# Stored expert weights of the first layer: one transfer for two value steps, and five row slots instead of six

## The chip, the cores and the metric

The kernel runs on one core of one Trainium2 chip. The metric is device time in microseconds, the median of the runs. A profiled execution is a run of its own, with its own time.

## What is computed

A first block of two layers and a second block follow each other; the change lies in the first block's retrieval of single-neuron experts. With `n` tokens of width 1024, 8 heads, 16 choices each and 16384 experts:

```python
q = (hb @ w_q).reshape(n, PEER_HEADS, 2, PEER_DK_HALF)
s = jnp.einsum('nhpk,pek->nhpe', q, keys)
v_top, i_top = lax.top_k(s, PEER_TOPK)
...
e = i1 * N_KEYS + i2
g = jax.nn.softmax(sc.astype(jnp.float32), axis=-1).astype(hb.dtype)
a = jax.nn.gelu(jnp.einsum('nhkd,nd->nhk', u_tab[e], hb)) * g
return jnp.einsum('nhk,nhkd->nd', a, v_tab[e])
```

In the first layer this is done for 512 tokens (256 of the input, 256 of the context), in the second for the 256 of the input.

## The kernel before, in words

The kernel doesn't gather experts token by token. `peer` (L1694) computes the scores of all 16384 experts for all tokens, multiplies them with a dense matrix that holds the softmax weight where an expert was chosen and zero elsewhere, and multiplies the result with all of `peer_v`. Everything is float32, split into a high and a low half, so each product is three matmuls.

Its loops, each over tiles of 256 experts (`U` = 64 of them), with one block of instructions per engine, written out in order:

- Score steps: PE multiplies a tile of `peer_u` with the tokens, ACT applies the gelu, SP stores the scores in DRAM (`K.scores`). Beside that, DVE picks the best 16 and builds the dense weights, which go to DRAM in blocks of tokens (`K.dense`).
- Value steps, `m` = 0 to 63. SP fetches a tile of `peer_v` (1 MB, `fetch`, L1838), the scores of the step (`pr_gs`, L1863) and the dense weights of the step (`pr_g`, L1864). DVE multiplies scores and weights (`multiply`: L2303 twice to add two halves, L2305), ACT rounds the product to its high half (`split_a`, L2131) and the value tile to its high half (`split_hi`, L2061), DVE makes the low halves (`split_v`, L2314, and L2344), and PE accumulates (`combine`): in the first layer 36 matmuls of 512 columns.

In the first layer (`parts` is true) the value steps treat 384 of the 512 tokens. The first 128 are done by gathering: POOL gathers their 128 chosen scores (`gather_score`, L1919) and then the 128 chosen rows of `peer_v` for each token, one row per token and gather, 512 KB at a time (`gather_value`, L1925), and DVE adds them up with their weights (`sum_value`, L2331), 128 sums spread over steps 8 to 63, two or three per step.

The dense weights of the first layer lie in 12 blocks of 32 tokens. For each block `b` and each of the 128 partitions `j`, `K.dense[b, j, :]` is a row of 8192 numbers, and the 128 numbers of a step are 512 B of it.

What sets the order: each engine runs its own list. SP's list in the value steps is, for each `m`, first the scores and weights of step `m + 2` (`fetch_weighted`), then the value tile of step `m + ring`. In the first layer `ring` is 3, and its wait (`used`) is for the end of `combine(m)`. So after the end of `combine(m)` the value tile, the scores and the weights of step `m + 3` are issued together. `fetch_weighted` waits until the step three before has been multiplied (`mulled`), since there are three slots of scores and three of weights. DVE's list per step: multiply, split the value tile, the sums, the low half of the product; DVE counts both transfers of a slot on one semaphore (`sg_in`). POOL's list alternates a value gather and a score gather; a value gather into a slot that was used before waits for the sum that read it (`v_summed`), with six slots.

Of the kernel before, what the change touches and what calls it, by code (L numbers as in the profile page):

```python
# [9 lines left out]
ALU = mybir.AluOpType  # L10
# [4 lines left out]
P = 128  # L15
# [19 lines left out]
PH, TOPK, NKEYS = 8, 16, 128  # L35
# [16 lines left out]
@contextmanager  # L52
def stage(K, *names):


    nc = K.nc
    turn = K.stages % 2
    K.stages += 1
    sems = K.sems[turn][0:len(names)]
    retired = K.sems[1 - turn]  # L60
    with nc.Block(no_gpsimd_drain=True) as block:  # L61
        @block.gpsimd
        def _(pool):
            pool.sem_clear(range(retired[0].num, retired[-1].num + 1))
        yield (block, *sems)
# [1628 lines left out]
def peer(K, l, hT, x, t0, held):  # L1694
# [14 lines left out]
    parts = pairs == 2  # L1709
# [19 lines left out]
    nb = dw // stored  # L1729
# [9 lines left out]
    def ada_after(m):  # L1739
        return m - ada_from if ada_from <= m < ada_from + n_ada else None  # L1740
# [4 lines left out]
    with ExitStack() as mem:  # L1745
        def sb(name, shape, dt=F32, scope=mem):
            return scope.enter_context(nc.sbuf_tensor(f"pr_{name}{l}", shape, dt))
        act_s = sb("s", [P, 3, 2, tw])
        n_sel, v_slots, first_sum = PH * TOPK, 6, 8
        if parts:  # L1750
            sel_w = sb("sel_w", [P, n_sel])
            sel_row, sel_score = sb("sel_row", [P, n_sel], U32), sb("sel_score", [P, n_sel], U32)
# [38 lines left out]

        aslots = 2
        gs = sb("gs", [P, 3, 2, dw])
        gw = sb("g", [P, 3, nb, 2 * 64])
        a = sb("a", [P, aslots, 2, dw])
        a2 = sb("ahi", [P, aslots, 2, dw], F32R), sb("alo", [P, aslots, 2, dw], F32R)
        tail = ExitStack()
# [6 lines left out]
        if parts:  # L1804
# [4 lines left out]
                 "step", "shifted", "exped", "picked", "turned", "chosen", "hots_made", "hots_hi", "hots_lo", "paired", "copied",  # L1809
                 "g_stored0", "g_stored1", "s_stored0", "s_stored1", "s_stored2", "ada_in0", "ada_in1", "row_ready", "row_copied",  # L1810
                 "row_stored0", "row_stored1", "mod_in", "sg_in0", "sg_in1", "sg_in2", "v_lo", "mulled", "a_hi", "a_lo", "used", "outed", "scaled", "rows_in",
                 "selected", "sel_in0", "sel_in1", "sel_in2", "sel_in3", "v_in0", "v_in1", "v_in2", "v_in3", "v_in4", "v_in5", "v_summed"]
        with stage(K, *names) as \
                (block, w_in0, w_in1, w_in2, w_in3, keys_in, hi_ready, lo_ready, lo_later, scored, freed, key_scored, sc_copied, topped,
                 step, shifted, exped, picked, turned, chosen, hots_made, hots_hi, hots_lo, paired, copied,
                 g_stored0, g_stored1, s_stored0, s_stored1, s_stored2, ada_in0, ada_in1, row_ready, row_copied,
                 row_stored0, row_stored1, mod_in, sg_in0, sg_in1, sg_in2, v_lo, mulled, a_hi, a_lo, used, outed, scaled, rows_in,
                 selected, sel_in0, sel_in1, sel_in2, sel_in3, v_in0, v_in1, v_in2, v_in3, v_in4, v_in5, v_summed):
            w_in, g_stored, s_stored = (w_in0, w_in1, w_in2, w_in3), (g_stored0, g_stored1), (s_stored0, s_stored1, s_stored2)
            ada_in, row_stored, sg_in = (ada_in0, ada_in1), (row_stored0, row_stored1), (sg_in0, sg_in1, sg_in2)  # L1820
            sel_in, v_in = (sel_in0, sel_in1, sel_in2, sel_in3), (v_in0, v_in1, v_in2, v_in3, v_in4, v_in5)
            chunk = n_sel // len(sel_in)

            @block.sync
            def _(sp):
# [33 lines left out]
                def fetch_weighted(m):  # L1859
                    sp.wait_ge(s_stored[m % 3], 16 * (m // 3 + 1))  # L1860
                    if m >= 3:
                        sp.wait_ge(mulled, m - 2)
                    sp.dma_start(gs[:, m % 3, :, :], K.scores[m, :, 0:2 * tw].rearrange("p (e t) -> p e t", e=2)[:, :, off:tw]).then_inc(sg_in[m % 3], 16)  # L1863
                    sp.dma_start(gw[:, m % 3, :, :], K.dense[0:nb, :, m * 128:(m + 1) * 128].rearrange("b j n -> j b n")).then_inc(sg_in[m % 3], 16)  # L1864

                sp.dma_start(keys[:, :, :], K.dram["peer_keys"][l]).then_inc(keys_in, 16)
                lag = PH + 1 + ring
                for n in range(ring, first_v + lag - PH):
                    if n < first_v + ring:
                        fetch(n)  # L1870
                    m = n - lag
# [11 lines left out]
                    c = ada_after(m + lead)  # L1883
                    if c is not None:
                        fetch_ada(c)
                    c = ada_after(m)
# [6 lines left out]
                for m in range(U):  # L1893
                    if m + 2 < U:
                        fetch_weighted(m + 2)
                    if first_v + m + ring < first_v + U:
                        fetch(first_v + m + ring)
                    if m == U - 8 and not nxt:
                        sp.dma_start(x[:, 0:2, :], K.dram["mem"].rearrange("(t p) d -> p t d", p=P)).then_inc(rows_in, 16)
                    if m == 4:  # L1900
                        for s in range(2):
                            sp.dma_start(mod5[:, s, :], K.ada[l, s:s + 1, 5 * D:6 * D].broadcast_to([P, D])).then_inc(mod_in, 16)
# [4 lines left out]
            @block.gpsimd  # L1907
            def _(pool):
                def split_lo(n):
                    s = n % slots  # L1910
                    pool.wait_ge(hi_ready, n)
                    pool.tensor_tensor(w_lo[:, n % ring, :, :], wt[:, n % ring, :, :], w_hi[:, s, :, :].bitcast(F32),  # L1912
                                       ALU.subtract).then_inc(lo_ready, 1)

                for n in range(1, on_pool):
                    split_lo(n)

                def gather_score(j):
                    pool.indirect_dma_start(sel_s[:, j:j + 1], None, K.scores.rearrange("m p (n o) -> (m p n) o", o=1),  # L1919
                                            bass.IndirectOffsetOnAxis(ap=sel_score[:, j:j + 1], axis=0)).then_inc(sel_in[j // chunk], 16)  # L1920

                def gather_value(j):
                    if j >= v_slots:
                        pool.wait_ge(v_summed, j - v_slots + 1)
                    pool.indirect_dma_start(v_rows[:, j % v_slots, :], None, K.dram["peer_v"][l],  # L1925
                                            bass.IndirectOffsetOnAxis(ap=sel_row[:, j:j + 1], axis=0)).then_inc(v_in[j % v_slots], 16)

                if parts:
                    pool.wait_ge(selected, 1)
                    pool.wait_ge(row_copied, n_ada)  # L1930
                    for s in range(2):
                        pool.wait_ge(g_stored[s], 16 * (nb // 2))
                    for s in range(3):
                        pool.wait_ge(s_stored[s], 16 * ((U + 2 - s) // 3))
                    for j in range(chunk):
                        gather_score(j)
                    for j in range(n_sel):
                        gather_value(j)
                        if j + chunk < n_sel:
                            gather_score(j + chunk)  # L1940
# [227 lines left out]
            def _(dve):  # L2168
# [123 lines left out]
                            make_hots(g)  # L2292

                def multiply(m):
                    dve.wait_ge(sg_in[m % 3], 32 * (m // 3 + 1))
                    if m >= aslots:
                        dve.wait_ge(a_hi, m - aslots + 1)
                        dve.wait_ge(a_lo, m - aslots + 1)
                    if parts:
                        sums = a[:, m % aslots, :, :].rearrange("p e (b t) -> p b e t", t=stored)  # L2300
                        both_halves = gw[:, m % 3, :, :].rearrange("p b (e h t) -> p b e h t", e=2, h=2)
                        for e in range(2):
                            last = dve.tensor_tensor(sums[:, :, e, :], both_halves[:, :, e, 0, :], both_halves[:, :, e, 1, :], ALU.add)  # L2303
                        chain(last)
                        dve.tensor_tensor(a[:, m % aslots, :, :], a[:, m % aslots, :, :], gs[:, m % 3, :, :], ALU.mult).then_inc(mulled, 1)  # L2305
                        return
                    dve.tensor_tensor(a[:, m % aslots, :, :].rearrange("p e (b t) -> p e b t", t=64),
                                      gs[:, m % 3, :, :].rearrange("p e (b t) -> p e b t", t=64),
                                      gw[:, m % 3, :, :].rearrange("p b (e t) -> p e b t", t=64), ALU.mult).then_inc(mulled, 1)

                def split_v(m):
                    n = first_v + m
# [3 lines left out]

                def weigh(c):
                    cols = slice(c * chunk, (c + 1) * chunk)
                    dve.wait_ge(sel_in[c], 16 * chunk)
                    chain(dve.tensor_tensor(sel_a[:, cols], sel_w[:, cols], sel_s[:, cols], ALU.mult))  # L2320

                def sum_value(j):
# [28 lines left out]
                for o in range(outs):  # L2351
                    t, c = divmod(o, 2)
# [99 lines left out]
def first_layer(K, l, x, s_cols, cmp_bias):  # L2452
# [6 lines left out]
    with ExitStack() as mem:  # L2459
# [16 lines left out]
        with ExitStack() as rows:  # L2476
# [14 lines left out]
            with ExitStack() as over:  # L2491
# [3 lines left out]
        merge_out(K, l, x, (yT, y_lo), room, gm[:, :, :].rearrange("p (s a) c -> p s (a c)", s=2), ft[:, :, :].rearrange("p t c -> p (t c)"), hT, tiles, streams,  # L2495
                  held.ahead(K.dram["peer_w_q"][l]))
        peer(K, l, hT, x, t0, held)


# [1351 lines left out]
```

## Time and profile before

| | |
|---|---|
| time, median of 3 runs | 4358.7 us (4357.69 to 4365.27) |
| profiled execution, its own time | 4376.78 us |
| its span | 4375.0 us |
| PE busy | 3984.4 us (91%) |
| DVE busy | 2747.7 us (63%) |
| ACT busy | 1756.1 us (40%) |
| POOL busy | 786.5 us (18%) |
| DMA, whole span | 858.34 MB in 520773 packets, mean 196 GB/s |

Busy time is that of an engine's own instructions; issuing a DMA isn't counted as busy. An engine's idle time carries the name of what ended it. The granted clock of TensorE is 1.00 at 2.4 GHz and 0.50 at 1.2 GHz. The DMA share is the time that packets took on the 16 DMA engines together; it can be a little over 1 in a short stretch.

### The profile page before, as it was taken

Reading aid. Unit: us, or ns where it says so; the run is one execution under the profiler, and the core shown is the slowest. Engines: PE = TensorE matmul, PEld = TensorE weight load, DVE = VectorE, ACT = ScalarE, POOL = GpSimd, SP = SyncE. Lnnn points to the kernel's source line nnn. Section 1 sums busy time; section 2 is a strip of 40 time slices with the busy share of each in tenths; the row PEclk is TensorE's granted clock in tenths of the full one; section 3 lists DMA queues with packets and bytes.
Section 4 is the critical chain, followed back from the end, with each engine's and each line's share of the span. In section 5 each row is a group of like instructions: output and inputs, shape, how many; then the busy total and the mean of one; then the engine's idle time right before and its main releaser. Section 6 shows DMA issues by size and latency. Waiting matters only on the chain. (4 is left out here: it accounts for less than half of the span.)

```text
span 4375.0 us, 61084 instructions
## 1 busy us (share of the span) xinstructions
PE 3984.4 (91%) x24438; PEld 3468.0 (79%) x24438; DVE 2747.7 (63%) x5244; ACT 1756.1 (40%) x2260; POOL 786.5 (18%) x386
## 2 busy tenths in 40 slices
PE   7999899999999888878889899999997988888798
PEld 5876788788878767666778899997887977878697
DVE  5725668899412577777765688745665745643664
ACT  3433233477433222222255444544444523543453
POOL 2222034200000655542243320000000030000000
PEclk9999999999999989988899999999998979998999
DMA  6421224377884999999444366778885401645264
GB/s 244 141 94 60 93 87 136 125 287 298 315 286 157 295 304 329 339 323 300 135 135 140 139 202 218 250 281 279 288 290 172 154 1 58 190 144 162 71 188 138
DMA packets 520773, 858.34 MB, mean 196 GB/s; under 512 B 26661, under 2 KB 388325, under 8 KB 499721
## 3 DMA queue, kind: packets, MB, share of 16 engines
q1 hardware_dynamic: 497962, 787.25, 53.7%
q0 software_dynamic: 22528, 67.19, 4.3%
q8 instruction: 194, 3.18, 0.3%
q14 instruction: 89, 0.73, 0.1%
HBM read 734.21 MB, written 120.14 MB: 195 GB/s over the span
## 5 line engine op out<-in xcount | busy, mean ns | idle before, releaser
L113 PE MATMUL bank<-hThi_l,pr_whi 128*128 128x512 f32 (+1 forms) x2304 | 785.5, 341 | 17.1 <-DVE pr_wlo L2179 6.9
L113 PE MATMUL bank<-hTlo_l,pr_whi 128*128 128x512 f32 (+1 forms) x2304 | 777.7, 338 | 0.0
L113 PE MATMUL bank<-hThi_l,pr_wlo 128*128 128x512 f32 (+1 forms) x2304 | 777.2, 337 | 0.0
L113 PE MATMUL bank<-pr_whi,pr_ahi 128*128 128x512 f32 x1280 | 518.8, 405 | 116.9 <-DVE pr_alo L2344 113.6
L2061 ACT ACTIVATE pr_whi<-pr_w 128x2048 fp32r<-128x2048 f32 x270 | 516.3, 1912 | 133.3 <-DMA pr_w<-peer_v_in 130.6
L113 PE MATMUL bank<-pr_wlo,pr_ahi 128*128 128x512 f32 x1280 | 513.9, 401 | 0.0
L113 PE MATMUL bank<-pr_whi,pr_alo 128*128 128x512 f32 x1280 | 513.0, 401 | 0.0
L113 PEld LDWEIGHTS bank<-hThi_l,pr_whi 128*128 128x128 f32 x2304 | 440.3, 191 | 67.0 <-POOL pr_wlo L1912 8.3
L113 PEld LDWEIGHTS bank<-hThi_l,pr_wlo 128*128 128x128 f32 x2304 | 439.6, 191 | 45.9
L113 PEld LDWEIGHTS bank<-hTlo_l,pr_whi 128*128 128x128 f32 x2304 | 440.4, 191 | 42.7
L2179 DVE TENSOR_TENSOR pr_wlo<-pr_w,pr_whi 128x2048 fp32r<-128x2048 f32 x102 | 233.5, 2290 | 339.6 <-ACT pr_whi L2061 339.4
L113 PEld LDWEIGHTS bank<-pr_whi,pr_ahi 128*128 128x128 f32 x1280 | 250.4, 196 | 182.9 <-issue 115.9
L2075 ACT ACTIVATE pr_s<-bank 128x512 f32<-128x512 f32 (+1 forms) x256 | 125.2, 491 | 522.9 <-PE bank L113 505.6
L2131 ACT ACTIVATE pr_ahi<-pr_a 128x768 fp32r<-128x768 f32 (+1 forms) x128 | 94.7, 740 | 554.8 <-DVE pr_a L2305 250.4
L2314 DVE TENSOR_TENSOR pr_wlo<-pr_w,pr_whi 128x2048 fp32r<-128x2048 f32 x128 | 292.4, 2284 | 17.6 <-ACT pr_whi L2061 17.6
L113 PEld LDWEIGHTS bank<-pr_whi,pr_alo 128*128 128x128 f32 x1280 | 249.7, 195 | 54.3
L113 PEld LDWEIGHTS bank<-pr_wlo,pr_ahi 128*128 128x128 f32 x1280 | 250.8, 196 | 52.1
L1919 POOL DMA_INDIRECT pr_sel_s<-expert_scores,pr_sel_score x128 | 151.7, 1185 | 647.5 <-issue 647.5
L1912 POOL TENSOR_TENSOR pr_wlo<-pr_w,pr_whi 128x2048 fp32r<-128x2048 f32 x40 | 187.8, 4696 | 375.8 <-ACT pr_whi L2061 375.8
L1925 POOL DMA_INDIRECT pr_v_rows<-peer_v_in,pr_sel_row x128 | 180.5, 1410 | 262.6 <-DVE pr_v_sum L2331 237.0
L113 PE MATMUL bank<-b_fThi,gu_whi 128*128 128x256 f32 x704 | 200.3, 285 | 10.3 <-PEq L61 10.3
L113 PE MATMUL bank<-hThi_l,gr_whi 128*128 128x512 f32 (+1 forms) x512 | 189.0, 369 | 20.8 <-PEq L61 9.6
(617 smaller groups left out, 8815.6 us busy)
## 6 DMA issues: line engine op xcount, KB each, us to landing
pr_w<-peer_u_in SPq DMA_DIRECT2D x128, 1024.0 KB, 5.4
pr_w<-peer_v_in SPq DMA_DIRECT2D x128, 1024.0 KB, 5.1
dense_weights<-pr_buf SPq DMA_DIRECT2D x16, 4096.0 KB, 16.7
pr_g<-dense_weights SPq DMA_DIRECT2D x64, 768.0 KB
gu_w<-ffn_w_up_in SPq DMA_DIRECT2D x88, 512.0 KB, 4.8
gr_w<-w_in_in SPq DMA_DIRECT2D x32, 1024.0 KB, 5.3
expert_scores<-pr_s SPq DMA_DIRECT2D x64, 512.0 KB, 6.9
pr_ada_w<-w_ada_in SPq DMA_DIRECT2D x14, 2048.0 KB
```

The lines of the kernel that those rows point to most:

```text
L113: ins = pe.matmul(psum, a, b, start=first and i == 0, stop=last and i == len(terms) - 1)
L1912: pool.tensor_tensor(w_lo[:, n % ring, :, :], wt[:, n % ring, :, :], w_hi[:, s, :, :].bitcast(F32), ALU.subtract).then_inc(lo_ready, 1)
L1919: pool.indirect_dma_start(sel_s[:, j:j + 1], None, K.scores.rearrange("m p (n o) -> (m p n) o", o=1), bass.IndirectOffsetOnAxis(ap=sel_sco ...
L1925: pool.indirect_dma_start(v_rows[:, j % v_slots, :], None, K.dram["peer_v"][l], bass.IndirectOffsetOnAxis(ap=sel_row[:, j:j + 1], axis=0)) ...
L2061: act.activation(w_hi[:, n % slots, :, :], wt[:, n % ring, :, :], ACT.Copy).then_inc(hi_ready, 1)
L2075: act.activation(act_s[:, m % 3, j, :], K.ps[i % 4][:, 0:tw], ACT.Gelu_apprx_tanh).then_inc(freed, 1)
L2131: act.activation(a2[0][:, m % aslots, :, :], a[:, m % aslots, :, :], ACT.Copy).then_inc(a_hi, 1)
L2179: dve.tensor_tensor(w_lo[:, n % ring, :, :], wt[:, n % ring, :, :], w_hi[:, n % slots, :, :].bitcast(F32), ALU.subtract).then_inc(lo_later, 1)
L2314: dve.tensor_tensor(w_lo[:, n % ring, :, :], wt[:, n % ring, :, :], w_hi[:, n % slots, :, :].bitcast(F32), ALU.subtract).then_inc(v_lo, 1)
```

## The change

In the first layer the weights of two value steps come in one transfer, so that a row of it is 1 KB; two slots of that size take the place of three single ones. The transfer is issued with the scores of the even step. It has semaphores of its own (`gw_in`), and DVE waits for it and for the scores separately. The slots of gathered rows go from six to five. The four semaphores of the gathered scores become two, each used for two of the four groups of 32. In the second layer `gsteps` is 1 and `gslots` 3, as before, with the separate semaphores.

```diff
-        n_sel, v_slots, first_sum = PH * TOPK, 6, 8
+        n_sel, v_slots, first_sum = PH * TOPK, 5, 8
...
-        gw = sb("g", [P, 3, nb, 2 * 64])
+        gsteps, gslots = (2, 2) if parts else (1, 3)
+        gw = sb("g", [P, gslots, nb, gsteps * 2 * 64])
...
-            sel_in, v_in = (sel_in0, sel_in1, sel_in2, sel_in3), (v_in0, v_in1, v_in2, v_in3, v_in4, v_in5)
-            chunk = n_sel // len(sel_in)
+            sel_in, gw_in, v_in = (sel_in0, sel_in1), (gw_in0, gw_in1, gw_in2), (v_in0, v_in1, v_in2, v_in3, v_in4)
+            chunk = n_sel // 4
...
                     sp.dma_start(gs[:, m % 3, :, :], K.scores[m, :, 0:2 * tw].rearrange("p (e t) -> p e t", e=2)[:, :, off:tw]).then_inc(sg_in[m % 3], 16)
-                    sp.dma_start(gw[:, m % 3, :, :], K.dense[0:nb, :, m * 128:(m + 1) * 128].rearrange("b j n -> j b n")).then_inc(sg_in[m % 3], 16)
+                    if m % gsteps == 0:
+                        k = m // gsteps
+                        if k >= gslots:
+                            sp.wait_ge(mulled, (k - gslots + 1) * gsteps)
+                        sp.dma_start(gw[:, k % gslots, :, :], K.dense[0:nb, :, m * 128:(m + gsteps) * 128].rearrange("b j n -> j b n"))\
+                          .then_inc(gw_in[k % gslots], 16)
...
-                                            bass.IndirectOffsetOnAxis(ap=sel_score[:, j:j + 1], axis=0)).then_inc(sel_in[j // chunk], 16)
+                                            bass.IndirectOffsetOnAxis(ap=sel_score[:, j:j + 1], axis=0)).then_inc(sel_in[j // chunk % 2], 16)
...
                 def multiply(m):
-                    dve.wait_ge(sg_in[m % 3], 32 * (m // 3 + 1))
+                    k, part = divmod(m, gsteps)
+                    dve.wait_ge(sg_in[m % 3], 16 * (m // 3 + 1))
+                    dve.wait_ge(gw_in[k % gslots], 16 * (k // gslots + 1))
+                    weights_of = gw[:, k % gslots, :, part * 128:(part + 1) * 128]
...
-                        both_halves = gw[:, m % 3, :, :].rearrange("p b (e h t) -> p b e h t", e=2, h=2)
+                        both_halves = weights_of.rearrange("p b (e h t) -> p b e h t", e=2, h=2)
...
-                    dve.wait_ge(sel_in[c], 16 * chunk)
+                    dve.wait_ge(sel_in[c % 2], 16 * chunk * (c // 2 + 1))
```

## Rows read from the trace of the kernel before

**Rows 1.** The page's slices of the span: DMA engines, and the clock that PE was granted

```profile
PEclk9999999999999989988899999999998979998999
DMA  6421224377884999999444366778885401645264
```

**Rows 2.** Busy time of the engines in two stretches; columns in the first line

```profile
core 0: us, PE busy (x) PEld busy (x) DVE busy (x) ACT busy (x) POOL busy (x), PEclk, DMA share, GB/s
1490.00:2075.00 585.00, 482.57 (x1944) 389.18 (x1945) 429.36 (x403) 149.56 (x110) 291.44 (x223) 0.90 0.97 322
2950.00:3300.00 350.00, 339.62 (x1498) 279.56 (x1497) 216.30 (x185) 153.42 (x127) 0.00 (x0) 0.99 0.84 283
```

**Rows 3.** What SP's queue waited for, 1400 to 2100 us

```profile
SPq L1838 <- PE bank L113: 510.8, 60, 16.0
```

**Rows 4.** Timeline of SP's queue: start, duration of the issue, what is issued

```profile
1489.87 0.37 SPq L1838 DMA_DIRECT2D pr_w<-peer_v_in  x1
...
1606.47 0.37 SPq L1838 DMA_DIRECT2D pr_w<-peer_v_in  x1
...
1607.52 0.60 SPq L1864 DMA_DIRECT2D pr_g<-dense_weights  x1
1614.63 0.64 SPq L1838 DMA_DIRECT2D pr_w<-peer_v_in  x1
...
1622.79 0.37 SPq L1838 DMA_DIRECT2D pr_w<-peer_v_in  x1
...
1640.42 0.37 SPq L1838 DMA_DIRECT2D pr_w<-peer_v_in  x1
...
2075.39 0.37 SPq L1838 DMA_DIRECT2D pr_w<-peer_v_in  x1
```

**Rows 5.** Timeline of DVE, 1621 to 1629 us, idle time before in brackets

```profile
1621.31 1.03 DVE L2303 TENSOR_TENSOR pr_a<-pr_g 128x384 f32<-128x384 f32 x2 [9.24 <-DMA pr_g<-dense_weights]
...
1628.03 0.95 DVE L2344 TENSOR_TENSOR pr_alo<-pr_a,pr_ahi 128x768 fp32r<-128x768 f32 x1
1628.90 1.02 DVE L2303 TENSOR_TENSOR pr_a<-pr_g 128x384 f32<-128x384 f32 x2
```

**Rows 6.** Timeline of PE: the first matmul after a pause

```profile
1629.13 0.77 PE L113 MATMUL bank<-pr_whi,pr_ahi 128*128 128x512 f32 x1 [6.37 <-DVE pr_alo L2344]
```

**Rows 7.** Stretches of 2 us within one cycle; columns as in rows 2

```profile
1620.00:1622.00 2.00, 2.00 (x11) 1.65 (x10) 0.69 (x2) 0.00 (x0) 0.00 (x0) 1.00 1.01 401
1624.00:1626.00 2.00, 0.00 (x0) 0.00 (x0) 2.00 (x2) 1.58 (x2) 0.00 (x0) 0.74 1.16 308
1630.00:1632.00 2.00, 2.00 (x6) 1.52 (x6) 2.00 (x2) 1.05 (x2) 1.43 (x2) 0.50 1.15 314
1636.00:1638.00 2.00, 2.00 (x11) 1.65 (x10) 1.97 (x4) 0.00 (x0) 1.55 (x2) 1.00 0.35 80
```

**Rows 8.** Who waited for whom, 1411 to 2100 us: in total, times, longest

```profile
POOL pr_v_rows L1925 <- DVE pr_v_sum L2331: 237.0, 44, 13.8
DVE pr_a L2303 <- DMA pr_g<-dense_weights: 170.6, 36, 10.0
ACT pr_whi L2061 <- DMA pr_w<-peer_v_in: 130.6, 41, 8.2
...
PE bank L113 <- DVE pr_alo L2344: 103.2, 25, 9.3
...
DVE pr_v_sum L2331 <- DVE pr_v_sum L2331: 0.9, 2, 0.5
```

**Rows 9.** DMA queues, 1440 to 2080 us: packets, MB, share of 16 engines

```profile
q1 hardware_dynamic: 126610, 135.99, 66.5%
```

**Rows 10.** The same, 2950 to 3300 us, second layer

```profile
q1 hardware_dynamic: 58042, 98.88, 83.3%
```

**Rows 11.** Who waited for whom, 2948 to 3320 us, second layer

```profile
DVE pr_a L2307 <- DMA pr_g<-dense_weights: 132.3, 61, 7.1
...
PE bank L113 <- DVE pr_alo L2344: 10.4, 4, 4.4
```

More of the change, by code:

```diff
@@ L1811, in peer @@
                  "row_stored0", "row_stored1", "mod_in", "sg_in0", "sg_in1", "sg_in2", "v_lo", "mulled", "a_hi", "a_lo", "used", "outed", "scaled", "rows_in",
-                 "selected", "sel_in0", "sel_in1", "sel_in2", "sel_in3", "v_in0", "v_in1", "v_in2", "v_in3", "v_in4", "v_in5", "v_summed"]
+                 "selected", "sel_in0", "sel_in1", "gw_in0", "gw_in1", "gw_in2", "v_in0", "v_in1", "v_in2", "v_in3", "v_in4", "v_summed"]
         with stage(K, *names) as \
@@ L1817, in peer @@
                  row_stored0, row_stored1, mod_in, sg_in0, sg_in1, sg_in2, v_lo, mulled, a_hi, a_lo, used, outed, scaled, rows_in,
-                 selected, sel_in0, sel_in1, sel_in2, sel_in3, v_in0, v_in1, v_in2, v_in3, v_in4, v_in5, v_summed):
+                 selected, sel_in0, sel_in1, gw_in0, gw_in1, gw_in2, v_in0, v_in1, v_in2, v_in3, v_in4, v_summed):
             w_in, g_stored, s_stored = (w_in0, w_in1, w_in2, w_in3), (g_stored0, g_stored1), (s_stored0, s_stored1, s_stored2)
             ada_in, row_stored, sg_in = (ada_in0, ada_in1), (row_stored0, row_stored1), (sg_in0, sg_in1, sg_in2)
-            sel_in, v_in = (sel_in0, sel_in1, sel_in2, sel_in3), (v_in0, v_in1, v_in2, v_in3, v_in4, v_in5)
-            chunk = n_sel // len(sel_in)
+            sel_in, gw_in, v_in = (sel_in0, sel_in1), (gw_in0, gw_in1, gw_in2), (v_in0, v_in1, v_in2, v_in3, v_in4)
+            chunk = n_sel // 4
             @block.sync
@@ L2308, in multiply @@
                                       gs[:, m % 3, :, :].rearrange("p e (b t) -> p e b t", t=64),
-                                      gw[:, m % 3, :, :].rearrange("p b (e t) -> p e b t", t=64), ALU.mult).then_inc(mulled, 1)
+                                      weights_of.rearrange("p b (e t) -> p e b t", t=64), ALU.mult).then_inc(mulled, 1)
                 def split_v(m):
```

## The prediction

> **What bounds the kernel now.** I read the page's slices first, then the stage that the change touches, then its waits. From the fourteenth slice of the span to the nineteenth the DMA digit stands at 9, and in three of these six the granted TensorE clock falls to 8 [rows 1]: a stretch where transfers, not matmuls, set the pace. Cut to the value steps of the first layer with the whole load on (1490 to 2075 us), the 16 DMA engines are busy 97% of the time, while PE is busy 482.6 of 585 us at a mean clock of 0.90; the same loop in the second layer has PE at 339.6 of 350 us and DMA at 0.84 [rows 2]. So only the first layer's loop has anything to give.
>
> One step of it: when PE ends a combine, SP is let go and issues at once the value tile (L1838), the scores (L1863) and the stored weights (L1864) of three steps later. SP spends 510.8 us in 60 waits for PE there [rows 3], so each L1838 stamp marks the end of a combine. From the stamp at 1489.87 to that at 2075.39 lie 54 steps [rows 4]: 10.84 us each. A combine that waits for nothing takes 8.16 us (1606.47 to 1614.63 [rows 4]). The loop loses 2.68 us per step, 145 us in all.
>
> The loss isn't spread evenly. Stamps run 8.16, 8.16 and then 17.63 us [rows 4]. Take this cycle. The batch issued from 1606.47 lets DVE start its multiply only at 1621.31, after 9.24 us of idling for the stored weights [rows 5]: 14.8 us. From there to the end of the low half of `a` (1628.03 + 0.95) it is 7.7 us. PE starts at 1629.13 after 6.37 us of idling [rows 6], at half clock (0.50 at 1630; this is 1.2 instead of 2.4 GHz, and it fell while PE stood still) [rows 7], and ends at 1640.42: 11.3 us for a combine of 8.16. So a cycle of three steps costs 14.8 + 7.7 + 11.3 = 33.9 us. In the sums DVE waits 170.6 us for the weights in 36 waits, ACT 130.6 us for value tiles, PE 103.2 us for the low half [rows 8]. The chain is: transfer, DVE, PE.
>
> **The price of a packet.** The stored weights of one step are 12 blocks x 128 partitions of 512 B: 1536 packets, against 256 of 4 KB for the value tile and 256 of 1.5 KB for the scores. Two stretches give two equations for queue 1. In 1440 to 2080: 66.5% of 16 x 640 us = 6810 us for 126,610 packets and 135.99 MB [rows 9]. In 2950 to 3300: 83.3% of 16 x 350 = 4665 us for 58,042 packets and 98.88 MB [rows 10]. They solve to 8.4 ns per packet and 42.2 ns per 1000 B. One step then costs, over 16 engines: value tile 256 x 181 ns = 2.90 us, scores 256 x 73 ns = 1.17, weights 1536 x 30.0 ns = 2.88, and 128/56 = 2.29 gathered blocks of 128 rows at 181 ns = 3.32. Sum 10.27 us of the step's 10.84, or 95%, beside the row's 97% [rows 2]: the price list holds together.
>
> **The change, part by part.**
> - *Two steps in one transfer.* Again 1536 packets, now of 1 KB: 8.4 + 43.2 = 51.6 ns each, 4.96 us for two steps instead of 5.76. That is 0.40 us per step, 25.8 us over 64. This is an estimate between 512 B and longer packets. Bounds: nothing, if bytes alone count; and, if 1 KB ran as well as the longest packets, 786 KB at 397 instead of 265 GB/s (401 GB/s at share 1.01, when value tiles and rows move by the order of issue; 308 at 1.16, when weights do [rows 7]), 0.98 us per step or 63 us. I take the 0.40, since 1 KB is nearest to the short end.
> - *When it is asked for.* The double transfer goes with the even step's scores; its wait (both steps of the pair two back are multiplied) asks for the same count as the scores' wait just before it. Nothing is asked for later; the odd step's weights come a step earlier. But batches become uneven: even 2.90 + 1.17 + 4.96 = 9.03 us, odd 4.07, where each was 6.95. The heavy one is 2.08 us longer, the light one 2.88 shorter. What queues behind the heavy one is the next value tile, which ACT waits for.
> - *Five row slots.* Row j is asked for after sum j-5 instead of j-6. POOL idles for those sums already (237.0 us in 44 waits), and DVE waited for rows 0.9 us in all [rows 8]. Per cycle it is still seven rows on the same seven sums, so the load on DMA keeps its rhythm; a row has one sum (1.28 us) less to land. Between a sum and the fifth after it lie two steps, over 15 us. I take nothing. The cover is that slack; if rows were only just in time, a sum's 1.3 us in each of 56 steps would cost 73 us. No reason for a gain.
> - *Semaphores.* DVE's multiply waits on four instead of three. Now its start (1628.90) lies no later than the end of the work before it (1628.98) [rows 5], so a wait that is met doesn't show; on the 21 cycle heads 0.1 us each would be 2 us. Reused score semaphores count 32 gathers each and the later chunk is asked for long after the earlier is used: nothing. SP issues one DMA fewer every second step (0.60 us [rows 4]) on an engine that waits 510.8 us: nothing.
> - *The second layer* keeps one step per transfer and three slots, with one more wait per step on SP (already met) and DVE. PE waits there 10.4 us in 4 waits, and DVE's 132.3 us for weights are hidden behind PE [rows 11]: nothing.
>
> **The sum.** A step's service falls from 10.27 to 9.87 us. At the same fullness the step goes from 10.84 to 10.42, 23 us over the 54 steps; with the ten steps outside that stretch up to 4 more, less 2 for the waits: 25 us. The profiled execution took 4376.78 us (span 4375.0), 18 us above the median of 4358.7, so 4352 there; carried to the median, 4334 us. What is late next is the heavy batch, and PE keeps stalling, less.
>
> A rule against this: the Trainium skill, "DMA: Bandwidth & Descriptors", Specifications, gives 512 B as the smallest transfer at line rate; by it the packets already run at full rate, the first term is zero and the time stays at 4359. The trace differs: the full engines moved 308 GB/s in one stretch and 401 in another [rows 7].
>
> **Rivals.**
> - *The rhythm breaks (more is gained), 19%.* If a light batch heads the cycle, DVE gets it at least 2.9 us sooner, and PE's 6.4 us of idling and the 3.1 us of half clock shrink together: 9.5 us per such cycle, nine of 18 cycles, is 86 us, less 2.08 x 9 = 19 for the heavy ones. That would pass the DMA floor of 9.87 us per step, which allows 52. Say 45: 4314. For it: DMA has slack inside a cycle (share 0.35 at 1636 [rows 7]). Against: value rows fill what comes free.
> - *Bytes decide, or the transfer isn't cut as it says (no change), 16%.* If the rate is that of memory and contention, halving the packets gives 0, and 4359. The same if 1 KB still went as two packets. For: 322 GB/s over the stretch, 283 in the less full one [rows 2]. Against: the price list above.
> - *The heavy transfer in front (slower), 9%.* Place: the batch that heads a cycle. If it is heavy in half of 20 cycles, 10 x 2.08 = 21 us are added; the light ones give nothing back if their value tile, behind the heavy transfer, ends last (ACT's 130.6 us [rows 8]). Time 4380. It decides from the point where light cycles gain under 2.1 us.
> - *Rows late for want of a slot (slower), 3%.* A third of the bound above: 4383.
>
> **How the numbers follow.** The forecast's own case has 53%, 4318 to 4352. About 0.2% (9 us) is what a measurement can tell. Faster: 0.53 less 0.02 for its edge, plus 0.19 = 0.70. Same: 0.16 and that edge, 0.18. Slower: 0.12. The range runs from 4303 (the DMA floor and a little) to 4362 (no change), leaving out the slower cases and some of the ends.
>
> **What would show it.** Right: packets of queue 1 in the stage fall by about 49,000 (64 x 768), its share of the engines by 25.8 us, DMA stays near 0.96 full, DVE's wait for weights falls below 170.6 us and now stands before even steps, stamps average about 10.4 us; DVE's waits for value rows stay near 1 us; the second layer's stretch unchanged. Wrong: packets down and the share not (bytes decide); even steps waiting longer and odd ones not shorter; waits of L2331 for rows; or stamps of 9.9 and a clock near 1 (the rhythm broke).

## The result, and the profile after

The changed kernel takes 4394.29 us (median of 9 runs, 4385.68 to 4418.82) against 4362.74 us of the kernel before (9 runs, 4346.71 to 4376.9): ratio 1.0079 with the interval 1.0057 to 1.0101. It is slower by some 34 us; 4334 and a gain were forecast. The profiled execution of before lies 14 us above its own median and that of the changed kernel at its own, so the two traces differ by less, 17.5 us of span (4375.0 to 4392.5).

Queue 1 on the page of the kernel before, then slices and queue 1 on the page of the changed kernel (packets, MB, share of 16 engines):

```profile
q1 hardware_dynamic: 497962, 787.25, 53.7%
```
```profile
PEclk8999999999999988988899999999998978998999
DMA  6421224377875898989443466678885401645264
...
q1 hardware_dynamic: 448298, 787.24, 52.9%
```

The DMA digits of the stage, which were all 9 [rows 1], now have 8 among them. Queue 1 has 49,664 packets fewer over the span than the 497,962 of before, at the same bytes. Its time on 16 engines goes from 53.7% of 4375.0 to 52.9% of 4392.5 us, from 2349 to 2324: 26 us less. The first term of the sum is there as time of the DMA engines (25.8 were forecast; each share is rounded to some 2 us). The same stretch as in [rows 2], and queue 1 as in [rows 9]:

```profile
1490.00:2075.00 585.00, 474.85 (x1939) 383.84 (x1937) 414.04 (x388) 144.20 (x106) 289.99 (x220) 0.90 0.92 316
```
```profile
q1 hardware_dynamic: 79354, 134.53, 60.9%
```

The engines of the DMA are less busy (0.92 instead of 0.97), they move less (316 instead of 322 GB/s), and PE did less too. Time was saved on the resource that was thought to set the pace, and the pace fell. The stamps of the value tiles (L1838 is now L1839), timeline of SP's queue, first and last of the same 54 steps as in [rows 4], and one stall between them:

```profile
1496.96 0.37 SPq L1839 DMA_DIRECT2D pr_w<-peer_v_in  x1
...
1704.55 0.38 SPq L1839 DMA_DIRECT2D pr_w<-peer_v_in  x1
1705.34 0.52 SPq L1864 DMA_DIRECT2D pr_gs<-expert_scores  x1
1705.92 0.69 SPq L1869 DMA_DIRECT2D pr_g<-dense_weights  x1
1712.71 0.37 SPq L1839 DMA_DIRECT2D pr_w<-peer_v_in  x1
1713.19 0.94 SPq L1864 DMA_DIRECT2D pr_gs<-expert_scores  x1
1720.87 0.38 SPq L1839 DMA_DIRECT2D pr_w<-peer_v_in  x1
...
1743.23 0.37 SPq L1839 DMA_DIRECT2D pr_w<-peer_v_in  x1
...
2094.92 0.37 SPq L1839 DMA_DIRECT2D pr_w<-peer_v_in  x1
```

54 steps take 598.0 us, 11.07 each instead of 10.84: 12.4 us more; the steps ahead of them lose another 4.3 (from the first stamp to the tenth, 87.3 instead of 83.0 us). The trace's loss lies in the value steps of the first layer. DVE's timeline says before which of them, by its starts of a multiply after a long pause:

```profile
1505.26 1.03 DVE L2312 TENSOR_TENSOR pr_a<-pr_g 128x384 f32<-128x384 f32 x2 [9.79 <-issue]
...
1549.89 1.03 DVE L2312 TENSOR_TENSOR pr_a<-pr_g 128x384 f32<-128x384 f32 x2 [9.44 <-issue]
...
1593.92 1.03 DVE L2312 TENSOR_TENSOR pr_a<-pr_g 128x384 f32<-128x384 f32 x2 [9.75 <-issue]
...
1637.48 1.03 DVE L2312 TENSOR_TENSOR pr_a<-pr_g 128x384 f32<-128x384 f32 x2 [10.76 <-issue]
...
1678.09 1.03 DVE L2312 TENSOR_TENSOR pr_a<-pr_g 128x384 f32<-128x384 f32 x2 [7.18 <-issue]
...
1722.76 1.03 DVE L2312 TENSOR_TENSOR pr_a<-pr_g 128x384 f32<-128x384 f32 x2 [11.54 <-issue]
```

Counted from step 0 these are steps 8, 12, 16, 20, 24 and 28: four apart, all even. Before, long pauses came every third step (10, 13, 16, 19, 22), even and odd in turn; step 19 is the 1621.31 of [rows 5], the others are these:

```profile
1522.02 1.03 DVE L2303 TENSOR_TENSOR pr_a<-pr_g 128x384 f32<-128x384 f32 x2 [8.93 <-DMA pr_g<-dense_weights]
...
1553.26 1.03 DVE L2303 TENSOR_TENSOR pr_a<-pr_g 128x384 f32<-128x384 f32 x2 [7.00 <-DMA pr_g<-dense_weights]
...
1587.49 1.03 DVE L2303 TENSOR_TENSOR pr_a<-pr_g 128x384 f32<-128x384 f32 x2 [9.99 <-DMA pr_g<-dense_weights]
...
1654.78 1.03 DVE L2303 TENSOR_TENSOR pr_a<-pr_g 128x384 f32<-128x384 f32 x2 [9.23 <-DMA pr_g<-dense_weights]
```

The waits of the stage in the changed kernel:

```profile
POOL pr_v_rows L1931 <- DVE pr_v_sum L2340: 246.6, 47, 13.7
DVE pr_a L2312 <- issue: 156.6, 24, 11.7
ACT pr_whi L2067 <- DMA pr_w<-peer_v_in: 155.6, 39, 6.7
PE bank L113 <- DVE pr_alo L2353: 125.2, 21, 11.1
...
DVE pr_a L2312 <- DMA pr_gs<-expert_scores: 37.1, 15, 5.1
```

The first DVE row (the profile names no transfer for it, and calls it issue) holds exactly the pauses before even steps, the second those before odd steps: 156.6 and 37.1 us, together 194. In the kernel before, it was 93.5 us ahead of even and 83.3 ahead of odd steps, together 177 (the 170.6 of [rows 8], and one pause of 6.2 that the profile calls issue). So even steps wait longer and odd ones shorter. The 17 us more are as much as the two traces differ by. PE's waits grow from 103.2 to 125.2 us. In the stall shown, the stamp at 1704.55 starts the heavy batch and DVE gets it at 1722.76: 18.2 us, against 14.8 in the cycle of the prediction. Over all pauses longer than 2.5 us from step 8 on, the mean time from stamp to multiply is 16.7 us before the even steps of the changed kernel (15 pauses) and 13.5 us in the kernel before (21 pauses, even and odd).

### The profile page after: what moved, and what is told of

It reads as the page before. It is cut to its first block and busy times, and to the rows that moved or that the text cites. A ratio compares the mean times of both kernels' runs of the same rounds, so it can differ in the third digit from the quotient of the medians.

```text
span 4392.5 us, 61180 instructions
## 1 busy us (share of the span) xinstructions
PE 3985.7 (91%) x24438; PEld 3467.0 (79%) x24438; DVE 2748.4 (63%) x5244; ACT 1755.5 (40%) x2260; POOL 789.3 (18%) x386
## 3 DMA queue, kind: packets, MB, share of 16 engines
q1 hardware_dynamic: 448298, 787.24, 52.9%
## 5 line engine op out<-in xcount | busy, mean ns | idle before, releaser
L2067 ACT ACTIVATE pr_whi<-pr_w 128x2048 fp32r<-128x2048 f32 x270 | 516.4, 1912 | 158.6 <-DMA pr_w<-peer_v_in 155.6
```

The source lines that it names most:

```text
L2067: act.activation(w_hi[:, n % slots, :, :], wt[:, n % ring, :, :], ACT.Copy).then_inc(hi_ready, 1)
```

## The experiments

Burst theory: the loss comes from asking for 1.5 MB in one go with a lead of three steps. Rivals: the fifth row slot (slots theory), and packets that cost nothing by themselves (bytes theory). Ratios are to the kernel before.

| kernel | what | ratio, interval |
|---|---|---|
| e1_slots5 | before, five row slots | 1.0002 (0.9979 to 1.0025) |
| e2_halves | 1 KB packets, even batches | 0.9952 (0.9935 to 0.9969) |
| e5_uneven512 | 512 B packets, uneven batches | 1.0092 (1.0063 to 1.0122) |
| e3_after_early | changed kernel, a step earlier | 0.9925 (0.9898 to 0.9951) |
| e4_before_early | before, a step earlier | 0.9888 (0.9865 to 0.9912) |
| h_early | 1 KB, even, a step earlier | 0.9844 (0.9820 to 0.9869) |
| e6_order | changed kernel, weights ahead of the value tile | 1.0120 (1.0093 to 1.0146) |

**Five slots alone.**

```diff
-        n_sel, v_slots, first_sum = PH * TOPK, 6, 8
+        n_sel, v_slots, first_sum = PH * TOPK, 5, 8
```

> The kernel before with five row slots instead of six and nothing else. Burst theory (the loss comes from asking for two steps' weights, 1.5 MB, in one go, with a lead of three steps): ratio to before 0.998 to 1.002, DVE's wait for value rows near 1 us. Slots theory (the fifth slot makes gathered rows late or bunches them): ratio 1.005 to 1.008, and waits of L2331 for rows, or a changed rhythm.

The time doesn't move, and DVE's pause before sums stays small. The group of L2331 in this trace (stage, by form):

```profile
L2331 DVE SCALAR_TENSOR_TENSOR pr_v_sum<-pr_v_rows,pr_sel_a,pr_v_sum 128x1024 f32<-128x1024 f32 x127 | 162.8, 1282 | 9.8 <-DMA pr_v_rows<-peer_v_in,pr_sel_row 1.5 <-DVE pr_v_sum L2331 0.9
```

1.5 us of waiting for rows in 127 sums. The slots theory is out. The same trace is a warning about single traces. From its tenth stamp to its last:

```profile
1493.10 0.37 SPq L1838 DMA_DIRECT2D pr_w<-peer_v_in  x1
...
2051.80 0.37 SPq L1838 DMA_DIRECT2D pr_w<-peer_v_in  x1
```

The 54 steps take 558.7 us, 10.35 each and not 10.84, though the medians are alike: this execution (4357.53 us) lies at its median, that of before 14 us above. Whether the slot or the execution makes the difference, one trace of each can't tell. Against this trace the steps of the changed kernel lose 39 us, not 12.

**Even halves.** In the changed kernel each call of `fetch_weighted(m)` asks for half of a pair's blocks:

```diff
-                    if m % gsteps == 0:
-                        k = m // gsteps
...
+                    for piece in ([0, 1] if m == 0 else [m + 1]):
+                        k, half_no = divmod(piece, 2)
...
-                        sp.dma_start(gw[:, k % gslots, :, :], K.dense[0:nb, :, m * 128:(m + gsteps) * 128].rearrange("b j n -> j b n"))\
+                        some = slice(half_no * nb // 2, (half_no + 1) * nb // 2)
+                        sp.dma_start(gw[:, k % gslots, some, :], K.dense[some, :, 2 * k * 128:(2 * k + 2) * 128].rearrange("b j n -> j b n"))\
...
-                    dve.wait_ge(gw_in[k % gslots], 16 * (k // gslots + 1))
+                    dve.wait_ge(gw_in[k % gslots], 16 * gsteps * (k // gslots + 1))
```

> The changed kernel, but each double transfer is cut by blocks of tokens: six of the twelve blocks go with the odd step before, six with the even step, so every batch has 768 packets of 1 KB and 786 KB, as even as before. Five row slots stay. Burst theory: the loss is gone; with the packet price of 51.6 ns the batch falls from 6.95 to 6.5 us, so ratio to before 0.992 to 0.999, stamps of the value tiles back to a rhythm of three steps. Slots theory: as the changed kernel, 1.005 to 1.010. Bytes theory (packets cost nothing): no loss and no gain, 0.999 to 1.002.

0.9952 is 21 us faster than before and 0.0127, or 55 us, faster than the changed kernel, with the same packets, slots, semaphores and bytes. What differs is that half of each pair's weights moves out of the heavy batch into the light one before it, which also means that this half is asked for a step earlier; the two can't be had apart here. So the semaphores, which weren't tried alone, aren't what made the changed kernel slow. That the gain over the kernel before is due to the packets isn't shown, because there too half of the weights come with more lead. Its waits (the execution profiled, 4361.23 us, is the slowest of its eleven):

```profile
DVE pr_a L2319 <- issue: 109.8, 23, 10.6
PE bank L113 <- DVE pr_alo L2360: 87.5, 22, 11.2
...
DVE pr_a L2319 <- DMA pr_gs<-expert_scores: 38.6, 14, 6.2
```

The waits before even steps fall by 47 us, those before odd steps stay. The mean time from stamp to multiply, counted as above, falls before even steps from 16.7 to 13.9 us. One part of the expectation missed: many pauses are still four steps apart. A likely reason, not tried, is that the pair, though asked for evenly, is still due as a whole at the even step.

**Uneven, with short packets.** The pair is asked for at the even step, in two transfers of 512 B packets:

```diff
-                        sp.dma_start(gw[:, k % gslots, :, :], K.dense[0:nb, :, m * 128:(m + gsteps) * 128].rearrange("b j n -> j b n"))\
...
+                        for i in range(gsteps):
+                            sp.dma_start(gw[:, k % gslots, :, i * 128:(i + 1) * 128], K.dense[0:nb, :, (m + i) * 128:(m + i + 1) * 128].rearrange("b j n -> j b n"))\
...
```

> The changed kernel with its double slots and its asking for two steps at the even step, but as two transfers of 512 B packets. Burst theory: all the unevenness and none of the saved packets; the heavy batch grows from 9.03 to 9.83 us by the packet price, so slower than the changed kernel by 10 to 30 us: ratio to before 1.010 to 1.016. Bytes theory: as the changed kernel, 1.006 to 1.010. Slots theory: 1.006 to 1.014, it does not tell.

1.0092 has no clear distance from 1.0079, so it doesn't tell burst from bytes; the burst theory's 1.010 to 1.016 was missed. It does say that packets aren't what made the changed kernel slow: with those of before it is as slow, and its long pauses too stand before even steps, four apart for long stretches (14, 18, 22, up to 38), 17.0 us after their stamps in the mean.

**A step more lead.** In the changed kernel and, the same edit, in the kernel before:

```diff
-                    if m + 2 < U:
+                    if parts:
+                        for later in ([2, 3] if m == 0 else [m + 3]):
+                            if later < U:
+                                fetch_weighted(later)
+                    elif m + 2 < U:
                         fetch_weighted(m + 2)
                     if first_v + m + ring < first_v + U:
                         fetch(first_v + m + ring)
```

> The changed kernel, but in the first layer scores and weights of step m+3 are asked for ahead of the value tile of step m+3 in SP's list, so that they no longer wait for PE to end combine m, only for DVE to have multiplied step m. Burst theory: the heavy transfer gets most of one step (up to 8 us) more lead, DVE's waits for it (about 190 us) fall by half or more, ratio to before 0.97 to 0.99. Slots theory: little changes, 1.004 to 1.010.

> The kernel before (512 B packets, one step per transfer, six row slots) with scores and weights of step m+3 asked for ahead of the value tile, as soon as step m is multiplied. Burst theory: a longer lead helps even batches too, but less than it helped the changed kernel (0.0154 from 1.0079 to 0.9925): ratio to before 0.990 to 0.999. Rival (the lead is what the kernel lacks, unevenness is nothing by itself): the lead helps both alike, 0.982 to 0.988.

In effect, what is asked for after the end of `combine(m)` is now the value tile of step `m + 3` and scores and weights of step `m + 4`. The uneven kernel gains 0.0154 by it, the even one 0.0112. The lead is short for both. That it is shorter for the uneven one, as the burst theory wants, isn't shown: the difference of 0.0042 is as large as its uncertainty, worked out from the intervals of the table and of the changed kernel. The waits of e3_after_early:

```profile
ACT pr_whi L2071 <- DMA pr_w<-peer_v_in: 339.8, 59, 13.9
...
PE bank L113 <- DVE pr_alo L2357: 68.9, 24, 6.6
...
DVE pr_a L2316 <- issue: 34.7, 11, 10.2
```

DVE's pauses for weights fall from 194 to 36 us, more than expected, and the time by less (0.9925 where at most 0.99 was expected): the value tile ends last now, ACT waits 339.8 us for it instead of 155.6. The value steps of e4_before_early, whose last stamp comes earlier: its tenth and last stamp, the stretch, and queue 1 on its page:

```profile
1494.64 0.37 SPq L1838 DMA_DIRECT2D pr_w<-peer_v_in  x1
...
2010.48 0.42 SPq L1838 DMA_DIRECT2D pr_w<-peer_v_in  x1
```
```profile
1490.00:2010.00 520.00, 471.59 (x1964) 379.36 (x1963) 426.54 (x399) 144.92 (x108) 296.14 (x228) 0.96 1.07 362
```
```profile
q1 hardware_dynamic: 497962, 787.25, 54.5%
```

Nothing but the order of SP's list differs from the kernel before: same packets, same bytes. The engines move 362 GB/s instead of 322 [rows 2], and a step takes 9.55 us. Queue 1's packets took 54.5% of 4318.0 us, 2353 us of 16 engines, against 2349 before: in the mean a packet took as long, and there were more of them at a time.

**Both together**, the halves with the edit above:

> Even halves of 1 KB packets and the early asking together. Burst theory: with enough lead evenness adds little to the changed kernel asked early (0.9925): 0.988 to 0.994. If the gains of evenness (0.0127) and lead (0.0154) added up: 0.980.

0.9844, 68 us faster than before by the ratio, and better than both kernels: 4290.98 us (median). The stage in its trace:

```profile
1490.00:1980.00 490.00, 452.89 (x1942) 367.20 (x1941) 422.57 (x394) 144.94 (x108) 309.96 (x227) 0.98 1.04 380
```

380 GB/s and a clock of 0.98; from the tenth stamp (1491.00) to the last (1981.81) a step takes 9.09 us. This execution (4281.94 us) is the fastest of its five, that of e4_before_early (4319.78) the slowest of its six, so the traces lie further apart than the medians do. Even halves are worth 0.0081 even with the longer lead (0.9925 to 0.9844), where the expectation said little; the full sum of the gains, 0.980, is not reached. Even halves of 1 KB lie 0.0044 below single steps of 512 B here (0.9888 to 0.9844) and 0.0048 without the lead (1 to 0.9952): the same 19 to 21 us twice. How much of that is the packets and how much the earlier asking of half a pair isn't shown.

**Weights ahead of the value tile**, behind the same wait for PE:

```diff
-                    if m + 2 < U:
+                    if parts and m == 0:
+                        fetch_weighted(2)
+                    if parts and m + 3 < U:
+                        sp.wait_ge(used, m + 1)
+                        fetch_weighted(m + 3)
+                    if not parts and m + 2 < U:
                         fetch_weighted(m + 2)
```

> The changed kernel; scores and weights of step m+3 go ahead of the value tile of step m+3 in the queue, but behind the same wait for the end of combine m. So the lead is unchanged and only the 2.9 us of the value tile are no longer in front of the heavy transfer. If the value tile in front is the cause: DVE's wait for weights falls by 2.9 us per cycle, ratio to before 0.996 to 1.003. If the cause is the late asking alone: value tiles now end last by as much (ACT's wait for them, 155.6 us, grows), 1.004 to 1.012.

```profile
ACT pr_whi L2072 <- DMA pr_w<-peer_v_in: 401.9, 59, 17.9
...
DVE pr_a L2317 <- issue: 96.3, 18, 11.7
```

DVE's wait before even steps falls from 156.6 to 96.3 us and ACT's rises from 155.6 to 401.9; the time is no better. What stands in front in the queue is not the cause: the batch as a whole comes late, and whichever part goes last is waited for.

## Why the prediction was wrong

- *The price of a packet was near, as time of the DMA engines.* 8.4 ns were forecast per packet, 25.8 us in all. Queue 1's time over the span (share times span) is 2349 to 2358 us in the four traces with 512 B packets and 2310 to 2324 us in the five with 1 KB: 26 us between the two kernels of this change, 36 in the mean of all. That 26 met the forecast so closely is luck. What the packets are worth in time of the kernel isn't shown: where they alone differ, 1.0092 (e5_uneven512) and 1.0079 can't be told apart. By the rule of 512 B as the smallest transfer at line rate (the Trainium skill, "DMA: Bandwidth & Descriptors", Specifications) this term is zero; these traces don't agree, by the 26 to 36 us of engine time.
- *Slots, semaphores and the second layer were right at nothing.* Five slots measured 1.0002; the semaphores are in the faster e2_halves too; PE's wait for the low half in the second layer is 9.7 us instead of 10.4. The prediction misread one row for the slots: the 0.9 us of [rows 8] are waits of a sum for the sum before it, not for rows. That view has no wait of DVE for rows; with five slots it was 1.5 us.
- *The step that failed is "At the same fullness the step goes from 10.84 to 10.42".* It took a DMA share of 0.97 for a bound, though [rows 7] has shares of 1.15 and 1.16. It wasn't one: with the order of SP's list alone changed, the same engines moved the same bytes in steps of 9.55 us (tenth to last stamp, 515.8 us) at a share of 1.07. The loop was bound by the lead: a batch is asked for when PE ends a combine and is needed three combines later, and the transfer, DVE's 7.7 us and PE make up the cycle, as the prediction's own sum of 33.9 us said. In such a loop a saving on the mean batch gives nothing while the batches that head the cycles grow, as here from 6.95 to 9.03 us by the prediction's own prices.
- *The rival that came true was mis-sized.* "The heavy transfer in front" had 9% and 21 us: 2.08 us in half of 20 cycles. The kernel lost 34 us to the kernel before, and 55 us to even halves, in which half a pair is also asked for earlier. Two things failed. The rhythm didn't stay at three steps with heavy and light heads in turn; it went to four, and the long pauses lie before even steps, so nearly every head is heavy and the light batches have nothing to give back (37.1 us of 194). And a head grows by more than its own service: 16.7 instead of 13.5 us in the mean, 3.2 us and not 2.08. That the rhythm settles on even steps is read from the traces; why it picks four was not tried.
- *The rival of the broken rhythm* (45 us gained) named a real reserve and the wrong key: h_early gains 68 us, but the most of it through the lead (0.0108 of 0.0156), and its steps of 9.09 us lie below the "floor" of 9.87. The price list held (queue 1's packets took 2353 us in e4_before_early, 2349 before); what failed is a share of 1 as the most, since the engines reach 1.07 over 520 us.

## What to carry to other kernels

A transfer joined from two saves packets, but it is due as a whole with its first half. In a loop where each batch is asked for late, the batch that heads a cycle sets its length, so split it into even pieces or ask for it earlier first. Before a busy share near 1 is taken for a bound, ask when the transfers are issued: a list in which one stream's wait for a slot stands ahead of another stream's asking holds back both. Here moving one call in the queue's list was worth 0.0112, and even halves of 1 KB without it 0.0048. And look at where the profiled execution lies among the times of its kernel: two traces of kernels with equal medians differed by 27 us in this stage.

## What the hardware showed that was not expected

A share of 0.97 of the DMA engines left room: the first layer's value steps went from 322 GB/s at 0.97 to 362 at 1.07 and 380 at 1.04 without a byte less. The share adds up the time that packets took, and it passes 1 over 520 us, so the packets of one engine overlap in the profile's records. They took no longer in the slower kernel of the same packets: 2349 us of 16 engines for queue 1 before, 2353 in e4_before_early. So a share near 1 didn't say that the engines were full.
